# Late expert searches in pieces between dot products, first scores after half of wq, and sample ticks kept for that stage

## The reference

```
h = layer_norm(ALPHA * x + mixer(x))            # attention and state-space branch, gates, W_out
q = (h @ wq) -> 8 heads x (2 x 128)
s1 = q[:, :128] @ keys1.T ;  s2 = q[:, 128:] @ keys2.T      # 8 heads x 128 each
v1, i1 = top16(s1) ;  v2, i2 = top16(s2)
top_s, pos = top16(v1[i] + v2[j])               # 16 of 256 pairs
expert = i1 * 128 + i2 ;  gate = softmax(top_s)
act = gelu(sum_d h * u[expert])                 # 8 x 16 = 128 experts a token
y = layer_norm(ALPHA * h + sum_k gate * act * v[expert])
```

## Time and profile before

| what | value |
|---|---|
| median of 3 runs | 2220.77 us (2218.44 to 2232.58) |
| profiled execution, its own time | 2218.71 us |
| its span | 2216.9 us |
| TensorE busy | 1743.0 us, 79% |
| VectorE busy | 1087.6 us, 49% |
| ScalarE busy | 438.5 us, 20% |
| GpSimd busy | 812.5 us, 37% |
| moved by DMA | 563.37 MB, mean 254 GB/s |

### The profile page before, as it was taken

How to read it: one execution, slowest core, us unless ns; L and a number is a source line. 1 busy time by engine, 2 the same in 40 slices (tenths; PEclk the granted TensorE clock), 3 DMA queues, 4 the chain that set the end, 5 groups by cost and what they waited for, 6 DMA issues and landing times.

```text
span 2216.9 us, 16426 instructions
## 1 busy us (share of the span) xinstructions
PE 1743.0 (79%) x5473; PEld 917.1 (41%) x5473; DVE 1087.6 (49%) x2554; ACT 438.5 (20%) x996; POOL 812.5 (37%) x776
## 2 busy tenths in 40 slices
PE   5969668887998868887989989835564878777786
PEld 5646434334863335454444444412222333333332
DVE  3443543122569566267222241596749544644543
ACT  0112111101111135232230221201121121122111
POOL 0000000000145443232232232346676777777773
PEclk9979889998999988988999999977887999888888
DMA  8711444664688764443766666467888999999996
GB/s 252 263 49 45 127 124 159 241 243 174 205 328 288 275 225 154 163 161 129 264 220 256 246 214 240 155 243 263 352 317 317 364 410 409 409 410 410 409 410 241
DMA packets 223356, 563.37 MB, mean 254 GB/s; under 512 B 20000, under 2 KB 73440, under 8 KB 222848
## 3 DMA queue, kind: packets, MB, share of 16 engines
q0 software_dynamic: 110736, 402.88, 48.1%
q1 hardware_dynamic: 112552, 159.63, 21.3%
HBM read 550.23 MB, written 12.23 MB: 254 GB/s over the span
## 4 chain that ended last, share of the span: by engine, by line
PE 51%; DVE 21%; DMA 10%; POOL 7%; ACT 5%; issue 5%; SPq 0%; DVEq 0%; ACTq 0%; POOLq 0%
PE bank L715 18%; PE bank L656 8%; POOL BIG L602 7%; PE bank L657 7%; PE bank L761 5%; DMA BIG<-in_peer_u_dram,BIG 4%; ACT BIG L1101 4%; DVE BIG L1435 3%; DMA wbuf<-in_w_in_dram 3%; PE bank L699 2%; PE bank L1034 2%; DVE BIG L1871 2%; DVE BIG L1868 1%; DMA out_s_ssm_dram<-BIG 1%; PE bank L855 1%
## 5 line engine op out<-in xcount | busy, mean ns | idle before, releaser
L602 POOL DMA_INDIRECT BIG<-in_peer_u_dram,BIG x384 | 427.8, 1114 | 1173.0 <-DVEq L1921 577.9
L656 PE MATMUL bank<-BIG 128*128 128x512 f32 x768 | 449.0, 669 | 260.3 <-ACT BIG L1101 236.0
L715 PE MATMUL bank<-wbuf,BIG 128*128 128x512 f32 x1056 | 463.5, 597 | 11.1 <-DMA wbuf<-in_w_in_dram 4.7
L602 POOL DMA_INDIRECT BIG<-in_peer_v_dram,BIG x384 | 381.7, 994 | 201.7 <-PE bank L657 111.5
L1951 DVE CUSTOM_DVE_ANT_0 BIG<-BIG 128x1024 f32<-128x1024 f32 x256 | 311.5, 1225 | 278.5 <-DMA BIG<-in_peer_u_dram,BIG 268.5
L657 PE MATMUL bank<-BIG 128*128 128x512 f32 x768 | 423.5, 635 | 0.0
L656 PEld LDWEIGHTS bank<-BIG 128*128 128x128 f32 x768 | 157.8, 213 | 478.4 <-issue 454.2
L715 PEld LDWEIGHTS bank<-wbuf,BIG 128*128 128x128 f32 x1056 | 200.7, 191 | 267.1 <-issue 247.7
L657 PEld LDWEIGHTS bank<-BIG 128*128 128x128 f32 x768 | 160.0, 208 | 214.1 <-issue 214.1
L1101 ACT ACTIVATE BIG<-bank 128x512 f32<-128x512 f32 (+5 forms) x211 | 102.9, 510 | 472.3 <-PE bank L761 160.2
L1101 ACT ACTIVATE BIG<-cst,small 128x128 f32<-128x128 f32 x384 | 122.5, 390 | 364.5 <-DVE small L1430 317.3
(11 more groups left out here) (167 smaller groups left out, 1226.2 us busy)
## 6 DMA issues: line engine op xcount, KB each, us to landing
wbuf<-in_w_in_dram SPq DMA_DIRECT2D x24, 2048.0 KB, 7.7
wbuf<-in_w_in_dram SPq DMA_DIRECT2D x16, 1536.0 KB, 7.8
wbuf<-in_w_ssm_br_dram SPq DMA_DIRECT2D x8, 2048.0 KB, 7.9
wbuf<-in_peer_wq_dram SPq DMA_DIRECT2D x8, 2048.0 KB, 8.0
wbuf<-in_w_attn_br_dram SPq DMA_DIRECT2D x4, 2048.0 KB, 7.9
BIG<-in_state_ssm_dram SPq DMA_DIRECT2D x16, 512.0 KB, 4.2
out_s_ssm_dram<-BIG SPq DMA_DIRECT2D x16, 512.0 KB, 3.7
wbuf<-in_w_out_dram SPq DMA_DIRECT2D x4, 2048.0 KB, 8.2
```

What stands on the lines that cost most here:

```text
L602: pool.indirect_dma_start(slot, None, table, bass.IndirectOffsetOnAxis(ap=eidx[:, col:col + 1], axis=0)).then_inc(done, 16)
L656: mm(acc[t][0][:, :], dg[:, j, :], slots[j][:, 0:512], start=False, stop=False, skip_group_check=True)
L715: last = mm(dst[:, :], lhs(b, k, toks[t]), wbuf[b][:, k, :], start=(k == 0), stop=(k == KC - 1))
```

## The change

**Ticks.** `TICKS_AT` gives fewer ticks to `conv`, `select`, `z`, `ym`, `gates` and `mixedT`, and more to `wq` and `scores`; a new place `late` has one. The total stays 66.

**First scores.** After two of the four wq products TensorE turns tile 0's first eight 128-column query pieces and makes their scores; VectorE copies these and starts `pick(0, 0)` while TensorE goes on with wq. Its pauses hold `pick`, `wq` and `scores` ticks; one pause (place 4) holds five. The scores of the other heads and of tile 1 follow after wq, and ScalarE copies them all. `pick(0, 1)` has the eight `late` ticks. The first search has a one-hot buffer of its own, since the usual one lies on `xT`, which wq still reads.

**Main loop.** The loops of VectorE and ScalarE are written out. `pick(1, 0)` runs beside turns 3 to 6 and `pick(1, 1)` beside turns 8 to 11: each of the eight pauses makes four dots. `finish(2)` moves behind turn 1's dots and `finish(0)` behind turn 18's. `dots8`, `gl8` and `w88` get two buffers. The weight of turn n-1 is issued after the first dot of turn n. The programs of POOL and SP and TensorE's main loop are not changed.

```diff
@@ -50,11 +50,13 @@
 PB = 8
 TURNS = P // PB
 PICK_STEPS = 8
+PICK_AT = {(1, 0): 3, (1, 1): 8}
+FINISH_AT = {2: 1, 0: TURNS + 2}
 ORDER = {2: 0, 0: 1, 1: 2}
 
-TICKS_AT = dict(pick=(1,), conv=(1,), dt=(0,), qkv=(1, 0, 1, 1), tails=(0,), rope=(1,), keys=(1,), select=(1,),
-                item1=(0,), item2=(1, 0), item3=(0,), ya=(1,), xbt=(0,), seg=(0,), y=(1,), z=(1,), yT=(1,), ym=(1,),
-                gates=(1,), mixedT=(1,), out=(0, 1), hT=(1,), wq=(1, 0), scores=(0,))
+TICKS_AT = dict(pick=(1,), late=(1,), conv=(1, 0), dt=(0,), qkv=(1, 0, 1, 1), tails=(0,), rope=(1,), keys=(1,), select=(1, 0),
+                item1=(0,), item2=(1, 0), item3=(0,), ya=(1,), xbt=(0,), seg=(0,), y=(1,), z=(1, 0), yT=(1,), ym=(1, 0),
+                gates=(1, 0), mixedT=(0,), out=(0, 1), hT=(1,), wq=(1,), scores=(1,))
...
@@ -360,10 +362,11 @@
                 self.phf, self.e1, self.e2 = tiny(128), tiny(128), tiny(128)
                 self.s8 = tiny(8)
                 self.cand = cand
-                self.hot = hot.rearrange("p (k j) -> p k j", j=PTOP)
-
-        late = Scratch(BIG[:, A + 2048:A + 2048 + 3584], BIG[:, A + 5632:A + 7680], PR.xT.rearrange("p k t -> p (k t)"))
-        scratch = {2: Scratch(PR.YD[:, 0:3584], PR.B[:, 2048:4096], BIG[:, PROMPT - 2048:PROMPT]), 0: late, 1: late}
+                self.hot = [h.rearrange("p (k j) -> p k j", j=PTOP) for h in hot]
+
+        late = Scratch(BIG[:, A + 2048:A + 2048 + 3584], BIG[:, A + 5632:A + 7680],
+                       [PR.C[:, 4096:6144], PR.xT.rearrange("p k t -> p (k t)")])
+        scratch = {2: Scratch(PR.YD[:, 0:3584], PR.B[:, 2048:4096], [BIG[:, PROMPT - 2048:PROMPT]] * 2), 0: late, 1: late}
...
-        dots8, gl8, w88 = tiny(PB), tiny(PB), tiny(PB)
+        dots8, gl8, w88 = ([tiny(PB) for _ in range(2)] for _ in range(3))
...
@@ -1041,35 +1044,49 @@
                         rows_to_T(htile(t), t, half)
                 s_written()
                 step("hT")
+                def scores(t, quarters, ring, bank):
+
+                    s_written()
+                    for quarter in quarters:
+                        rows_to_T(q.qp[:, L[t], :], t, quarter)
+                    s_written()
+                    for quarter in quarters:
+                        dst = bank()
+                        for i in range(4):
+                            last = mm(dst[:, i * P:(i + 1) * P], q.qT[:, 4 * quarter + i, :], keysT[:, i % 2, :],
+                                      start=True, stop=True)
+                        ring.give(last)
+
                 phase("wq")
-                products("wq", 2, x_part, sf, sbank)
-                phase("keysT")
                 if q.first:
+                    products("wq", 2, x_part, sf, sbank)
+                    phase("keysT")
                     pe.wait_ge(keys_in, 32)
                     dst = sbank()
                     for i in range(2):
                         last = turn(dst[:, i * P:(i + 1) * P], q.keys[:, i, :], ident)
                     sf.give(last)
-                phase("scores")
-                s_written()
-                for t in q.tiles:
-                    for quarter in range(4):
-                        rows_to_T(q.qp[:, L[t], :], t, quarter)
-                    s_written()
-
-                    for quarter in range(4):
-                        dst = sbank() if t == 1 else vbank()
-                        for i in range(4):
-                            last = mm(dst[:, i * P:(i + 1) * P], q.qT[:, 4 * quarter + i, :], keysT[:, i % 2, :],
-                                      start=True, stop=True)
-                        (sf if t == 1 else vf).give(last)
-                    step("scores")
+                    phase("scores")
+                    scores(2, range(4), vf, vbank)
+                else:
+                    products("wq", 1, x_part, sf, sbank)
+                    scores(0, (0, 1), vf, vbank)
+                    for b in range(2):
+                        for _ in range(2):
+                            step("pick")
+                        product("wq", b, x_part, sf, sbank)
+                        step("wq")
+                    for t, quarters in ((0, (2, 3)), (1, (0, 1)), (1, (2, 3))):
+                        scores(t, quarters, sf, sbank)
+                        step("scores")
+                    for _ in range(PICK_STEPS - 4):
+                        step("pick")
                 phase("end")
 
             mixer(ST)
             mixer(PR)
             for _ in range(PICK_STEPS):
-                steps.at("pick")
+                steps.at("late")
             places.append(steps.seen)
...
                             o = i * 1024 + (k * 2048 + b * 512)
                             sd.give(f(q.YD[:, o:o + 512], src[:, :]))
                         step("wq")
+                        if not q.first and (i, b) == (0, 1):
+                            keep_qT((0, 1))
                 if q.first:
                     src = bank()
                     sd.give(f(keysT, src[:, 0:256].rearrange("p (a n) -> p a n", a=2)))
-                for t in q.tiles:
-                    for quarter in range(4):
-                        src = bank()
-                        sd.give(f(q.qT[:, 4 * quarter:4 * quarter + 4, :], src[:, :].rearrange("p (c s) -> p c s", c=4)))
-                    if t == 1:
-                        for quarter in range(4):
...
-                dots_c.take(act)
-                f(gl8, dots8, ACT.Gelu).then_inc(gelu_done, 1)
-                w_c.take(act)
-                if used:
-                    vu.n += PB - 1
-                    vu.take(act)
+
+            for n in range(2 * TURNS):
+                if n == PICK_AT[1, 0] + 3:
+                    exp_scores(1, 0)
+                if n == PICK_AT[1, 1] + 3:
+                    exp_scores(1, 1)
+                act.wait_ge(dot8_done, PB * (n + 1))
+                f(gl8[n % 2], dots8[n % 2], ACT.Gelu).then_inc(gelu_done, 1)
+                for t in FINISH_AT:
+                    if n == FINISH_AT[t]:
+                        root(t, 1, var2_ready, root2_ready)
+                act.wait_ge(w_ready, BLOCKS + n + 1)
+                if n:
+                    act.wait_ge(v8_used, PB * n)
                 for j in range(PB):
-                    last = f(diag8[:, j, :], ident, scale=w88[:, j:j + 1])
+                    last = f(diag8[:, j, :], ident, scale=w88[n % 2][:, j:j + 1])
                 last.then_inc(diag_ready, 1)
-
-            def blocks(times):
-                with loop(act, times, (dots_c, PB), (w_c, 1), (vu, PB)):
-                    weigh(True)
-
-            weigh(False)
-            blocks(3)
-            exp_scores(1, 0)
-            blocks(4)
-            exp_scores(1, 1)
-            blocks(TURNS - 8)
-            blocks(2)
-            root(0, 1, var2_ready, root2_ready)
...
@@ -1849,17 +1865,25 @@
                     own.settle()
                     layer_norm(htile(t), htile(t), t, 0, q.ln1[:, 0, :], q.ln1[:, 1, :], var1_ready, root1_ready, h_ready)
                 step("hT")
-                for _ in range(4):
+                for _ in range(4 if q.first else 2):
                     step("wq")
 
 
-                for t in q.tiles[:1]:
-                    for quarter in range(4):
-                        src = bank()
-                        own(cp(sc[t][:, quarter * 512:(quarter + 1) * 512], src[:, :]), vd)
-                    own.settle()
-                for _ in q.tiles:
-                    step("scores")
+                for quarter in range(4 if q.first else 2):
+                    src = bank()
+                    own(cp(sc[q.tiles[0]][:, quarter * 512:(quarter + 1) * 512], src[:, :]), vd)
+                own.settle()
+                if not q.first:
+
+                    def between(place):
+                        if place in (2, 4):
+                            step("wq")
+                        if place == 4:
+                            for _ in range(3):
+                                step("scores")
+                        step("pick")
+
+                    pick(0, 0, between)
...
@@ -1935,32 +1959,39 @@
             own(nc.vector.memset(zero, 0.0))
             mixer(ST)
             mixer(PR)
-            pick(0, 0, lambda place: steps.at("pick"))
+            dve.wait_ge(sb_drained, SR + before[2, "end"][1])
+            pick(0, 1, lambda place: steps.at("late"))
             places.append(list(steps.seen))
             steps.run(TICKS)
-            pick(0, 1, lambda place: None)
-            finish(2)
-
-            landed = [Count(u_in[s], start=P // SLOTS if s < SLOTS else 0, step=16) for s in slot_sem]
-            gelu_c, w_c = Count(gelu_done, start=BLOCKS), Count(w_ready, start=BLOCKS)
-
-            def blocks(t, first, times):
-                with loop(dve, times, (gelu_c, 1), (w_c, 1), *((c, 1) for c in landed)) as i:
-                    for j in range(PB):
-                        landed[j].take(dve)
```

(42 more changed lines are left out.)

33 lines of the change are left out of this document (21 added, 12 removed).

## The result

The changed kernel takes 2389.49 us (median of 4 runs, 2384.87 to 2393.35), the kernel before on the same chip 2224.82 (2218.44 to 2232.58): ratio 1.0738, 95% interval 1.0694 to 1.0782. The profiled execution took 2390.32, its span is 2388.5; forecast were 2404 and 2400.

A forecast was written before the change was run, and what follows sets the result against it. TensorE, then VectorE, then full DMA engines (20.48 us a turn) bound the kernel; -8.7 front, -40.1 holes, +223.9 ring, +7.9 tail give +183.0: span 2400, time 2404 us, range 2335 to 2445, slower with chance 0.91.

The forecast's parts named there:

- Step 1: TensorE stages before wq: twelve sample ticks moved out save 33.7 us (bounds 28.3 to 41.3).
- T: Start time of the prompt wq product: 1341.2 us before, forecast 1307.5.
- Step 2: Tile 0 searches beside wq: start T+39, ends T+133 and T+181, with 31 us waiting for held-back u gathers.
- u(1,0): First u gather of turn 1 (turns are eight prompt rows, numbered 0 to 31); forecast at 1495.9 us instead of 1504.65.
- Step 3: Main loop: tile 1's searches in pieces close the holes they tear into the gather stream, saving 40.1 us over 29 turns.
- Step 4: Main loop: the late weight closes a one-turn ring of gather, dot, weight, rows, next gather: 28.2 us a turn against 20.48.
- Step 5: Last turn: its diagonals wait for the turn before, so TensorE starts 29.3 us after u(31,0) instead of 21.4: +7.9 us.
- A: Rival on the main loop: the ring has slack after all, only the gains stay, 2172 us; chance 0.07.
- B: Rival on the main loop: a shorter ring, clock up and landing 5.5 us, 25 us a turn, 2311 us; chance 0.08.
- C: Rival on the early search: it starves, main loop some 20 us later, 2424 us; sign u(1,0) after 1505; chance 0.15.
- The three stretches of the table: Span differences forecast: start to u(2,0) -8.7 us, 29 turns from u(2,0) to u(31,0) +183.8, u(31,0) to end +7.9.

The follow-up runs named there:

- Experiment 2: Changed kernel's front (fewer early ticks, early first scores and search) with the main loop of the kernel before: 2225.08 us, ratio 0.9977 to the kernel before.
- experiment 1: Changed kernel with only the weight put back right behind its own turn's eighth dot: 2197.04 us, ratio 0.9857 to the kernel before.
- experiment 3: Kernel before with the changed main loop alone, ticks and first scores as before: 2394.77 us, ratio 1.0756 to the kernel before.
- experiment 4: Changed kernel with the weight moved further back, behind the fifth dot of the next turn: 2597.18 us, ratio 1.1684 to the kernel before.
- experiment 5: Changed kernel, late weight kept, but POOL issues turn n+1's u gathers ahead of turn n's v gathers: 2200.05 us, ratio 0.9885 to the kernel before.
- Experiment 7: Changed kernel with half of each prompt row product on TensorE left out (output wrong): 2284.52 us, ratio 1.0257 to the kernel before.
- experiment 10: Experiment 1's kernel with prompt dots replaced by sums of the gathered row alone (output differs): 2178.15 us, ratio 0.9781 to the kernel before.

## Why the prediction was right

**Step 1, the ticks.** T was to be 1307.5. Timeline of PE of the changed kernel, start of the prompt wq product:

```profile
1308.11 4.45 PE L718 MATMUL bank<-wbuf,BIG 128*128 128x512 f32 x10
```

Within 0.6 us of the forecast, and that closeness is luck: in the ten profiled executions whose front is that of the changed kernel, wq starts between 1305.5 and 1317.2 us, 1313.0 on average, and the two with the front of before have 1341.2 and 1347.9. What the ticks gave is some 32 us by these means, forecast 33.7.

**Step 2, search beside wq.** Timeline of its DVE in the first search of tile 0 (L1892 is the search, L1446 a tick's weight, L1955 a search's last instruction):

```profile
1347.03 0.49 DVE L1892 MAX8 BIG<-BIG 128x8 f32<-128x128 f32 x2
...
1369.75 0.16 DVE L1446 TENSOR_TENSOR small<-small,BIG 128x2 f32<-128x2 f32 x1 [6.52 <-ACT small L1118]
...
1394.66 0.16 DVE L1446 TENSOR_TENSOR small<-small,BIG 128x2 f32<-128x2 f32 x1 [8.79 <-ACT small L1118]
...
1441.83 0.23 DVE L1955 TENSOR_TENSOR BIG<-BIG 128x64 f32<-128x64 f32 x1
...
1489.13 0.23 DVE L1955 TENSOR_TENSOR BIG<-BIG 128x64 f32<-128x64 f32 x1
```

Start at T+38.9 (forecast T+39), ends at T+134 and T+181 (forecast T+133 and T+181). The moments were right by luck, since the reason was wrong. The forecast had VectorE wait 31 us for u gathers held back by TensorE's ticks. It does wait 31.5 us between 1347 and 1490, but never for a gather: 29.3 us in five waits of 4.65 to 8.79 us end with ScalarE's Gelu, and 2.2 us with its exponential. Timeline of its ACT:

```profile
1393.36 0.60 ACT L1118 ACTIVATE BIG<-bank 128x512 f32<-128x512 f32 x1 [6.27 <-PE bank L718]
...
1394.44 0.19 ACT L1118 ACTIVATE small<-small 128x2 f32<-128x2 f32 x1
```

The Gelu of a tick (1394.44) stands in ScalarE's queue behind the copy of a bank that TensorE has to fill first, in two of the five waits by a wq product, in the other three by the turned queries and scores. No run changed that order.

What follows was off by 8 us. Timeline of its POOL, second half of turn 0 and the first u gathers of turns 1, 2 and 31:

```profile
1490.21 1.21 POOL L605 DMA_INDIRECT BIG<-in_peer_u_dram,BIG  x1 [1.84 <-PE bank L660]
1491.73 1.99 POOL L605 DMA_INDIRECT BIG<-in_peer_u_dram,BIG  x1 [0.30 <-issue]
...
1503.88 0.94 POOL L605 DMA_INDIRECT BIG<-in_peer_u_dram,BIG  x1 [0.30 <-issue]
...
1531.74 0.94 POOL L605 DMA_INDIRECT BIG<-in_peer_u_dram,BIG  x1 [0.30 <-issue]
...
2333.87 0.93 POOL L605 DMA_INDIRECT BIG<-in_peer_u_dram,BIG  x1 [0.30 <-issue]
```

u(1,0) came at 1503.88, forecast 1495.9. The second eight gathers of turn 0 start at 1490.21 and take 13.7 us instead of 8 x 1.24 = 9.9: they are issued beside VectorE's dots, which begin at 1489.39. That is 3.8 of the 8 us; the term that failed is the price of an issue, 1.24 us, which holds only where VectorE doesn't hold the issue up. The other 4 us are there before: TensorE's last tick ends at 1489.43, T+181.3 and not T+178.5, and POOL's first gather behind it starts 0.8 us later. Experiment 2 shows the outcome: the front is worth next to nothing.

**Step 3, the holes.** They closed: no turn between u(2,0) and u(31,0) of experiment 1 is longer than 24.6 us, where the earlier trace rows had 81.6 for three. But the 40.1 us were priced with turns of 20.48, and with pieces in them they take 22.09: twelve turns at 1.61 us, 19 us, are given back in experiment 1. In the changed kernel itself this is hidden inside the ring: its turns with pieces take 27.1 to 29.3 us, as the others do.

**Step 4, the ring.** Right in mechanism (experiments 1, 3, 4 and 5 each turn it on, up or off), and in size: 27.66 us a turn (802.1 over 29) for 28.2. By parts, as means of the 29 turns:

| link | forecast | measured |
|---|---|---|
| first u gather to first dot | 6.5 | 6.36 |
| dot | 1.15 | 1.15 |
| weight to TensorE's start | 2.86 | 2.78 |
| eight rows | 16.2 | 15.85 |
| last row to the next u gather | 1.5 | 1.53 |

The rows' term has the largest part of the miss, 0.35 of 0.54 us, and the landing 0.14. TensorE idles 11.3 to 12.9 us before each turn and then starts at its lower clock: in the turn shown the granted clock is 0.50 of full speed (1.2 GHz) from 2010.74 to 2012.70 and 1.00 (2.4 GHz) from 2014.00 on, and the two halves of row 0 take 2.07 and 1.54 us, each half from row 1 on 1.02. The forecast put the rows between the 15.69 us after 4.28 us of idle and the 16.85 after 47; the mean lies there too, nearer to the lower end. 29 x 0.54 is the 15.7 us between +168.1 and +183.8. Experiment 7 adds a limit that the prediction had not named: with half the rows' work POOL's eight issues take their place, and the turns still take 22.8 to 26.0 us.

The fit for one software DMA, which the prediction took from the Trainium skill (DMA: Bandwidth & Descriptors, the section on the anatomy of a software DMA), gives an estimate of 3.2 us for a gather and would have given a turn of 24.9; 6.36 us were measured on average from issue to first dot, with other gathers in flight.

**Step 5, the tail.** Timeline of its PE, the first row of turn 31:

```profile
2362.70 1.12 PE L659 MATMUL bank<-BIG 128*128 128x512 f32 x2 [2.67 <-ACT BIG L1118]
```

It starts 28.8 us after u(31,0), forecast 29.3. Only 2.67 us of idle lie ahead of it, and its rows take 14.0 us where the last turn of the kernel before had 15.7, which the forecast left out; hence +5.8 and not +7.9.

**Rivals.** A (slack) is refuted: the doubled dots, Gelu and weight did not help, since the v slots and POOL's order close the ring; experiment 5 shows what A would have needed. B's 25 us did not come: the landing is 6.36 us and not 5.5, the rows 15.85 and not 14.00. C's sign was a u(1,0) past 1505; it came at 1503.88. In the other profiled executions with this front and POOL's order it comes at 1503.76 to 1512.83, so that sign alone decides nothing; the searches ended where the forecast had them, and VectorE waits for no gather in them, so C's starved gathers do not appear.

The three stretches of the table missed by +6.4, -15.7 and -2.1 us. That the whole came within 11.4 us is in part because they cancel.

## What to carry to other kernels

When a step is put behind a wait, follow what it releases around to that wait: if the wait is for a transfer that is queued behind work which needs the step, the loop has become one serial ring, and its turn is the sum of the links, whatever slack each engine has. This ring could be cut at two of its links, by moving the step (experiment 1) or by reordering the transfers (experiment 5), and shortening one link helped only down to the next engine's own time (experiment 7). A search cut into pieces beside gathers isn't free even where VectorE idles half the time: price what it does to the engine that issues.

## What the hardware showed beside that

Gather issues on GpSimd take 0.94 us (1.24 from one to the next) beside an idle VectorE or one that runs sums over one SBUF operand, and up to 1.99 us in experiment 1 beside dot products of 1.22 us. An issue that begins while a dot product runs ends 0.81 us after it. The mean over 338 issues was 1.04 us in experiment 1 and over 353 issues 0.94 in experiment 10. The row shows no releaser: the time is inside the instruction, and nothing in experiment 1's list of POOL's waits names VectorE.

The Trainium skill (SBUF — State Buffer, the section on SBUF's two separate sides) has a rule for it: a VectorE instruction with two SBUF inputs takes a port pair that GpSimd shares, as an exclusive lock, against a GpSimd operation that reads SBUF; whichever starts first keeps the pair for its whole instruction and the other waits. The trace agrees: 1291 of 1329 gather issues that begin under a dot product end 0.79 to 0.83 us after it, and none of 58 is held beside instructions with one operand in SBUF and one in PSUM.

A turn of 20.48 us with a DMA share of 1.02 looked like the floor of the DMA engines. In experiment 10 six turns in a row ran at 19.87 (1754.79 to 1874.04). That is no lower floor: sixteen gathers of 0.524 MB in 19.87 us are 422 GB/s, and the engines moved 407 in that stretch, 410 in the later turns of 20.48. POOL issued ahead of them: from the first u gather to the first sum of a turn it took 6.08 us at 1754.79, 7.88 at 1814.41 and 9.49 at 2040.20. That this lead ends the fast turns was not tested.
